# A hybrid mixer layer on one core: branch inputs rounded inside the last inverse transform, branch projections on two sets of banks, arrays placed anew, the vector block loaded ahead of x

## The reference, cut to what matters

```python
h = rmsnorm(x, n1) * (1 + sc1) + sh1
u = h @ w_in                                   # 56 weight tiles of 1024 x 128
z = x1 * (fft_conv(v, kf[:, 0]) + bias[0] * v)  # Hyena, two orders, FFT over the sequence
z = x2 * (fft_conv(z, kf[:, 1]) + bias[1] * z)
y_a = z @ w_a                                  # Hyena branch, 512 channels in
y_b = fnet_branch(u_fn) @ w_b                  # FNet branch, 512 channels in
y_c = ((h_f + h_b) * gelu(u_ry)) @ w_c         # RG-LRU branch, 1024 channels in
x = x + g1 * ((ga * y_a + gb * y_b + gc * y_c) @ w_o)
h = rmsnorm(x, n2) * (1 + sc2) + sh2
x = x + g2 * ((silu(gt) * up) @ w_down)        # FFN
```

## Time and profile before

| what | value |
|---|---|
| median of 3 runs (lowest, highest) | 2621.64 us (2621.34, 2622.27) |
| the profiled execution | 2618.41 us, of which the span of the trace is 2616.5 us |
| PE busy in matmuls | 2477.3 us, 95% of the span |
| DVE, ACT, POOL busy | 55%, 24%, 26% |
| mean granted TensorE clock | 0.978 of full |
| DMA | 24.9% of 16 engines, 90 GB/s mean |

### The profile page before, as it was taken

How to read it: one execution, slowest core, us unless ns; L and a number is a source line. 1 busy time by engine, 2 the same in 40 slices (tenths; PEclk the granted TensorE clock), 3 DMA queues, 4 the chain that set the end, 5 groups by cost and what they waited for, 6 DMA issues and landing times. The chain is left out here.

```text
span 2616.5 us, 34805 instructions
## 1 busy us (share of the span) xinstructions
PE 2477.3 (95%) x13478; PEld 2099.3 (80%) x13478; DVE 1447.0 (55%) x2691; ACT 623.4 (24%) x887; POOL 688.2 (26%) x300
## 2 busy tenths in 40 slices
PE   4599999999997999999979989999999999999997
PEld 2488888867775888888868878888888888888886
DVE  5778786566585777776764383752233322332236
ACT  3423222565664222222220011310000000000004
POOL 1011111221212222322224452433134231432220
PEclk8799999999998999999989999999999999999999
DMA  7144443211115222322354242111011000111002
GB/s 297 48 172 156 166 161 117 82 40 61 60 40 190 99 99 98 116 98 98 118 204 148 66 166 82 49 33 46 19 48 48 32 32 32 48 40 40 24 24 81
DMA packets 53752, 234.24 MB, mean 90 GB/s; under 512 B 6131, under 2 KB 8755, under 8 KB 48068
## 3 DMA queue, kind: packets, MB, share of 16 engines
q1 hardware_dynamic: 53700, 233.54, 24.9%
HBM read 178.98 MB, written 54.53 MB: 89 GB/s over the span
## 5 line engine op out<-in xcount | busy, mean ns | idle before, releaser
L801 PE MATMUL ps<-h_hi,w_hi 128*128 128x512 f32 (+1 forms) x2112 | 760.3, 360 | 15.1 <-DVEq L1718 9.4
L803 PE MATMUL ps<-h_hi,w_lo 128*128 128x512 f32 (+1 forms) x2112 | 750.0, 355 | 0.0
L802 PE MATMUL ps<-h_lo,w_hi 128*128 128x512 f32 (+1 forms) x2112 | 750.0, 355 | 0.0
L759 POOL TENSOR_TENSOR w_hi<-w_raw,zero_col 128x1024 fp32r<-128x1024 f32 x96 | 205.5, 2140 | 1638.4 <-PE ps L803 1198.6
L801 PEld LDWEIGHTS ps<-h_hi,w_hi 128*128 128x128 f32 x2112 | 400.8, 190 | 77.0 <-DVEq L1718 9.8
L803 PEld LDWEIGHTS ps<-h_hi,w_lo 128*128 128x128 f32 x2112 | 400.4, 190 | 57.3
L802 PEld LDWEIGHTS ps<-h_lo,w_hi 128*128 128x128 f32 x2112 | 400.9, 190 | 56.5 <-issue 0.2
L2051 DVE TENSOR_TENSOR a<-sil,ps 128x512 f32<-128x512 f32 (+1 forms) x66 | 39.5, 599 | 504.1 <-PE ps L803 501.8
L762 POOL TENSOR_TENSOR w_lo<-w_raw,w_hi 128x1024 fp32r<-128x1024 f32 x96 | 262.3, 2732 | 7.5
L2074 DVE SCALAR_TENSOR_TENSOR x<-ps,mod,x 128x512 f32<-128x512 f32 (+1 forms) x264 | 172.3, 661 | 98.1 <-PE ps L803 97.5
L802 PE MATMUL ps<-h_lo,wf_hi 128*128 128x512 f32 (+1 forms) x624 | 224.3, 359 | 0.0
(11 more groups left out here) (276 smaller groups left out, 3500.3 us busy)
## 6 DMA issues: line engine op xcount, KB each, us to landing
w_raw<-in_weights SPq DMA_DIRECT2D x146, 512.0 KB, 3.9
ada_w<-in_w_ada SPq DMA_DIRECT2D x18, 1024.0 KB, 8.2
scratch_gate_s<-g_st SPq DMA_DIRECT2D x24, 640.0 KB, 3.3
side<-scratch_gate_s SPq DMA_DIRECT2D x24, 640.0 KB, 4.0
scratch_k_s<-kstage SPq DMA_DIRECT2D x8, 1536.0 KB, 6.6
hy_k<-scratch_k_s SPq DMA_DIRECT2D x8, 1536.0 KB, 8.7
scratch_hy_s<-hout SPq DMA_DIRECT2D x16, 640.0 KB, 3.2
ada_early<-in_w_ada SPq DMA_DIRECT2D x6, 1024.0 KB, 20.7
```

The costliest lines, as they stand in the source:

```text
L759: nc.gpsimd.tensor_tensor(hi[:], w_raw[slot % 2][:], zero_col[:].to_broadcast([P, D]), ALU.add).then_inc(pool_step, 1)
L801: mm(out, w_pair[0], x_pair[0], start=first, stop=False)
L802: mm(out, w_pair[0], x_pair[1], start=False, stop=False)
L803: return mm(out, w_pair[1], x_pair[0], start=False, stop=last)
```

## The change

What it does, part by part:

- **vec ahead of x.** The block of vectors `vec` (81 KB) is issued on SP ahead of the 8 tiles of x, instead of behind them.
- **Norm 1.** DVE multiplies both latent pieces of x by their roots ahead of the conditioning (8 tiles in each of two turns); ACT copies the root of the context piece to SBUF (`rstd_ctx`). So ps[1] and ps[2] come free early, and piece 1 is made as piece 0 is. ACT makes u of tiles 1, 3 and 5 of both latent pieces, DVE the others.
- **Arrays placed anew.** `v_b` and `g_st` lie where they can be written before RG-LRU has ended. `v_b` is loaded behind `inv`, ahead of the last chunk's `zc_ready`, and ACT's gate(0) of the first L3 pass waits for `xr_ready` instead of `zc_ready`; a new semaphore `xr_used` guards `ztok`.
- **z 0 to 3 in the last L3 pass.** The last pass is written apart from the loop on SP, ACT and DVE. SP loads z 2 (into `v_b`) and 3 (into a buffer of its own) behind `hy_k` of the last order, z 0 and 1 where it did, and the gates of jobs 0 and 1 behind the last inverse unit. ACT rounds the four in the order 2, 3, 0, 1 around its copies of the last inverse units, DVE takes their remainders ahead of its last inverse.
- **Two sets of banks.** Odd jobs use ps[3] to ps[5], with semaphores `other_done` and `other_free`. DVE takes job n-4 ahead of z n, where it took z n first.

```diff
+U_BY_ACT = [n < 2 * KD and n % KD in (1, 3, 5) for n in range(3 * KD)]
...
+        Z_ORDER = [2, 3, 0, 1] + list(range(4, 16))
...
+            return (other_free[b], u // 2 + 1) if u % 2 else (proj_free[b], use0 + u // 2 + 1)
...
+            sp.dma_start(vec[:], dr["vec"]).then_inc(vec_in, 16)
             sp.dma_start(x_in[:, 0, :], dr["x"][0]).then_inc(x_loaded[0], 16)
             sp.dma_start(cvec[:], dr["cvec"]).then_inc(cvec_in, 16)
             for k in range(1, KD):
                 sp.dma_start(x_in[:, k, :], dr["x"][k]).then_inc(x_loaded[k], 16)
-            sp.dma_start(vec[:], dr["vec"]).then_inc(vec_in, 16)
...
                         sp.dma_start(inv[:], dr["inv"]).then_inc(hy_const_in, 16)
+                        sp.dma_start(v_b[:], dr["hy_s"][0]).then_inc(v_in, 16)
                     sp.wait_ge(zc_ready, n + 2)
...
-            sp.dma_start(v_b[:], dr["hy_s"][0]).then_inc(v_in, 16)
             sp.dma_start(dr["state_out"], fin[:]).then_inc(fin_stored, 16)
...
+                    if order == 1 and last:
+                        load_z(2, dr["zb_s"][2])
+                        load_z(3, dr["zb_s"][3])
...
                             sp.wait_ge(y_ready, 4 * CH)
-                            for n in range(3):
+                            for n in range(2):
                                 load_z(n, dr["zb_s"][n])
+                            sp.wait_ge(mix_done[LAST_INVERSE[0]], LAST_INVERSE[1])
+                            for n in range(2):
+                                load_side(n, gate_src[n])
...
+            act.wait_ge(proj_done[2], 1)
+            fn(rstd_ctx, ps[2][:, 0:CTX], ACT.Copy).then_inc(proj_free[2], 1)
             act.wait_ge(norm_ready, 1)
...
-                        act.wait_ge(zc_ready, 1 + KD)
+                        act.wait_ge(xr_ready, 1 + KD)
                     gate(0)
 
+                    act.wait_ge(xr_used, KD)
...
                         if j == 2:
                             gate(2, (0,))
+                            if last and order == 1:
+                                round_z(2)
...
+                    if last and order == 1:
+                        for n in Z_ORDER[1:4]:
+                            round_z(n)
                     gate(2, (1, 2))
...
-                for k in ((), (0, 1, 2, 3), (4, 5, 6, 7), ())[r]:
-                    dve.wait_ge(x_loaded[k], 16)
-                    own.add(tt(x_in[:, k, 0:512], x_in[:, k, 0:512], ps[0], ALU.mult))
+                if r in (1, 2):
+                    p = r - 1
+                    a, e, _ = PIECES[p]
+                    dve.wait_ge(proj_done[p], 1)
+                    for k in range(KD):
+                        dve.wait_ge(x_loaded[k], 16)
+                        own.add(tt(x_in[:, k, a:e], x_in[:, k, a:e], ps[p], ALU.mult))
...
+                    if last and order == 1:
+                        dve.wait_ge(mix_done[LAST_INVERSE[0]], LAST_INVERSE[1])
+                        for n in Z_ORDER[0:4]:
+                            split_z(n)
                     for j in range(5):
                         mix_taken(u3, c, j0 + 9 + j)
...
-            for n in range(4):
-                split_z(n)
             for n in range(4, 12):
-                split_z(n)
                 take_branch(n - 4, n - 4)
+                split_z(n)
```

More of the change, by code:

```diff
@@ L388, in build_program @@
         inv = sb(st, "inv", [P, FH, 3, P])
+        v_b = sb(st, "v_b", [P, T])
+        x_b = sb(st, "x_b", [P, T])
         hy_y = sb(st, "hy_y", [P, 20, P])
-        x_b = sb(st, "x_b", [P, T])
-        v_b = sb(st, "v_b", [P, T])
+        g_st = sb(st, "g_st", [P, T])
         z_b = sb(st, "z_b", [P, T])
+        sb(st, "under_ztok", [P, 8])
         ztok = sb(st, "ztok", [P, FH, P])
@@ L463, in build_program @@
         mix_free = [sem(f"mix_free{b}") for b in range(MIX_BANKS)]
+        other_done = [sem(f"other_done{b}") for b in range(3)]
+        other_free = [sem(f"other_free{b}") for b in range(3)]
         act_step, dve_step = sem("act_step"), sem("dve_step")
@@ L666, in load_z, with load_side @@
                 sp.dma_start(buf[:], src).then_inc(loaded, 16)
+            def load_side(n, src):
+                if 2 <= n < 10:
+                    for b in range(3):
+                        sp.wait_ge(*branch_free(n - 2, b))
+                elif n >= 10:
+                    sp.wait_ge(side_used, n - 9)
+                sp.dma_start(side[n % 2][:], src).then_inc(side_in[n % 2], 16)
+            z_src = [dr["zb_s"][c] for c in range(4)] + [dr["zc_s"][n] for n in range(8)] + \
+                    [dr["za_s"][c] for c in range(4)]
+            gate_src = [dr["gate_s"][8 + m] for m in range(8)] + [dr["gate_s"][16 + m] for m in range(8)] + \
+                       [dr["gate_s"][m] for m in range(8)]
             def l3_pass(c, last):
@@ L1388, in _, with round_z, l3_pass @@
                     own.restart()
-            with act.Fori(0, CH) as c:
+            def round_z(n):
+                raw, loaded, count, _ = raw_z(n)
+                act.wait_ge(loaded, count)
+                dst = h_hi[:, n - 4, :] if 4 <= n < 12 else z2_hi[:, n % 12, :]
+                fn(dst, raw[:], ACT.Copy).then_inc(zhi_ready, 1)
+            def l3_pass(c, last):
                 for order in range(2):
@@ L1889, in _, with split_z, l3_pass @@
                     own.restart()
-            with dve.Fori(0, CH) as c:
+            def split_z(n):
+                at = Z_ORDER.index(n)
+                if n == 3:
+                    dve.wait_ge(z_split, at)
+                dve.wait_ge(zhi_ready, at + 1)
+                if 4 <= n < 12:
+                    hi, lo = h_hi[:, n - 4, :], h_lo[:, n - 4, :]
+                else:
+                    hi, lo = z2_hi[:, n % 12, :], z2_lo[:, n % 12, :]
+                tt(lo, raw_z(n)[0][:], hi.bitcast(F32), ALU.subtract).then_inc(z_split, 1)
+            def l3_pass(c, last):
                 for order in range(2):
@@ L1970, in split_merged @@
                 tt(h_lo[:, m, :], x1[:, m, :], h_hi[:, m, :].bitcast(F32), ALU.subtract).then_inc(m_split, 1)
-            for n in range(4):
+            for n in range(4, 12):
+                take_branch(n - 4, n - 4)
                 split_z(n)
-            for n in range(4, 12):
-                split_z(n)
-                take_branch(n - 4, n - 4)
             for n in range(12, 16):
@@ L1981, in _ @@
                 if m == 0:
-                    proj_taken(use0 + 7)
+                    for b in range(3):
+                        dve.wait_ge(*branch_free(7, b))
                 take_branch(8 + m, m)
```

171 lines of the change are left out of this document (89 added, 82 removed).

## The result

| what | value |
|---|---|
| changed kernel, median of 4 runs (lowest, highest) | 2591.54 us (2587.34, 2594.79) |
| kernel before, median of 4 runs beside it | 2621.49 us (2617.76, 2622.27) |
| ratio, 95% interval | 0.9888 (0.9874, 0.9903) |
| the profiled execution, its span | 2594.79 us, 2593.0 us |

What follows compares the result with a forecast made beforehand. PE, busy 2477.3 of 2616.5 us, bounds the kernel, leaving 139.2 idle to remove. Gains 13.4 + 1.5 + 12 + 4 = 30.9 against the median 2621.64 give 2590.7, stated as 2590.5; own range 2583 to 2598, wider range 2579 to 2604.

Steps and rivals of the forecast that it cites:

- Setup, 13.4: Setup up to PE's unit at 122.40: 9.9 from norm_a coming earlier plus 3.6 from piece 1, unit at 109.0.
- 11.5 earlier: Setup: ACT's ada_row starts at 43.9 and not at 55.37, because vec is loaded ahead of x.
- Start of L3, 1.5: Start of L3: the 16.56 wait on v_b goes, but the order's chain takes time back; gain 1.5 to 2, taken 1.5.
- All three links: Start of L3: DVE transforms 8.07 earlier, ACT's copy still held by gate's store, POOL's split costing 4 of 5.5.
- Jobs 0 to 7 and the wide entry, 12: Branch start: 18.3 wait and 1.9 slow clock gained, less 1.5, 3.3 and 2.4, and 1 for favourable estimates.
- Stalls 1.5 and 3.3: Branch start: PE waits 1.5 before job 2 (take behind z_b) and 3.3 before job 3 (behind z 4's remainder).
- The regained 1.9 of clock: Job 0: slow clock of 0.56 over the first 4 us goes with the removed wait, worth 1.9.
- Wide and last narrow jobs, 4: Four waits on side, 3.0 together, go with two sets of banks; with PE's refill 1 wide, 3 last narrow.
- B: Rival: all stalls close, with 10 at the start of L3 and 18 at the branch start; about 2576, chance 0.18.
- D: Rival: slower, load, rounding, remainder and take on each narrow job's path, 8.7 us each; about 2660, chance 0.03.
- C: Rival: setup gives less, terms 8, 0, 10.5 and 4, sum 22.5; 2599, chance 0.15.
- POOL in the inverse: Last inverse: POOL's w_hi blocked until DVE's chain ends, then meeting z_b; by the skill's rule time 2589.7 instead.

Runs made afterwards that it cites:

- v_late: Changed kernel with the first v_b load put back behind the last zc store; 2592.68 us, ratio 0.9896.
- all_three: Changed kernel with first L3 gate's store early, job 1 taken ahead of z 4's remainder, z 11's remainder ahead of job 7; 2576.12 us.
- gate_early: Changed kernel with the first L3 gate's store issued on SP ahead of the wait for zc_ready; 2585.65 us, ratio 0.9874.
- pool_hold: all_three with POOL's third split of the output projection's weights held until DVE has taken the last remainder; 2570.89 us, ratio 0.9811.

## Why the prediction was right, point by point

The forecast was 2590.5; measured were 2591.54 and 2593.32 in two sets of runs.

- **The sum.** Predicted 30.9. The table gives 23.5 and 25.8 for the two profiles; with setup at its mean of 13.0 in place of 9.5 the sum is 27.0. The medians differ by 30.0 and 26.2. Two figures in the working are off by 0.1: 9.9 + 3.6 is 13.5, and (1 - 0.56) x 4 is 1.8 where I put 1.9 for the slow clock. That the first median lies 1.0 from the forecast is in part luck: the kernel before read 2621.49 beside it and 2619.1 to 2619.7 in the later sets, and three of the four terms were off by 1 to 3, to either side, as follows.
- **Setup, 13.4.** 13.0 on average, 9.5 in the first profile. `vec` 11.4 and norm 1 1.6, against 11.5 and 2.0 by the prediction's own steps (the row 11.5 earlier; eight products a turn cost 1.6, piece 1 gives 3.6). In the first profile the step that failed is "11.5 earlier": `ada_row` came at 47.16, 8.2 earlier, 2.0 of the missing 3.3 because 20 matmuls for the sum of squares took 4.43 and not 2.39. PE's first unit, for which I named 109.0, started at 112.16. The second `reduce_angle` took 3.02 for 6.62, ahead of POOL, as said, and piece 1 gave 3.5 for 3.6. I had taken PE's own durations from before, where they hold a clock that isn't the same in each execution.
- **Start of L3, 1.5.** -0.3. All three links were there, and the inverse unit started at 853.36; setup gave 3.9 less than forecast, so that is 849.5 on the prediction's clock, for 849.2. The step that failed is the last: a wait of 7.68 in place of 0.27 ahead of the inverse unit brings the slow clock (0.50 for 4 us, some 2.0), which I had counted only as regained. The 1.6 gained at the unit are -0.3 at the next milestone.
- **Jobs 0 to 7 and the wide entry, 12.** 14.0 - 5.0 = 9.0. Job 0 18.3 earlier: right. Stalls 1.5 and 3.3: measured 1.93 and 2.13, for the reasons given. Mis-sized is the wide entry: 3.65 of wait and 1.4 of slow clock for 2.4, as POOL's split of the next tile met the remainder (2.94 for 1.49). The regained 1.9 of clock was spent again behind job 3's stall.
- **Wide and last narrow jobs, 4.** 0.6 + 4.5 = 5.1, of which 0.8 is PE's shorter wait at the output projection (3.7 for 4.5 in all), which I hadn't counted. It doesn't follow from the two sets alone: the last sum took 3.03 in before and 1.49 in changed, but 3.03 in v_late too, which gives 0.6 + 3.2 = 3.8.
- **Rivals.** B's 10 at the start of L3 was there for the taking, but only with the store moved, and not each time (8.8 in all_three, 3.5 and 3.2 in gate_early and pool_hold). D didn't come: load, rounding and remainder of the next z cost one stall of 2.13, at job 3. C's terms came nearest in the first profile: it had 8, 0, 10.5 and 4, sum 22.5, and that profile gave 9.5, -0.3, 9.0 and 5.1, sum 23.5. What speaks for the forecast is its setup term, 13.4 for an average of 13.0; C's setup was one end of a spread, and came at least in part by PE's longer matmuls.
- **POOL in the inverse.** I let POOL's `w_hi` be blocked until the chain ended. The chain in the changed kernel:

```profile
1303.92 0.28 DVE L219 TENSOR_TENSOR ztok<-hy_a 128x128 f32<-128x128 f32 x1
1304.12 0.22 DVE L225 TENSOR_SCALAR hy_a<-hy_a 128x128 f32<-128x128 f32 x1
1304.26 1.98 DVE L228 SCALAR_TENSOR_TENSOR hy_a<-hy_a 128x128 f32<-128x128 f32 x1
1306.16 0.21 DVE L225 TENSOR_SCALAR hy_a<-hy_a 128x128 f32<-128x128 f32 x1
1306.30 2.49 DVE L228 SCALAR_TENSOR_TENSOR hy_a<-hy_y,hy_a 128x128 f32<-128x128 f32 x1
```

POOL asked at 1302.83 and ended at 1306.09. Counted back by its 1.9 it began at 1304.2, at the first operation with one input (L225, 1304.12), and it ended 8 us ahead of the chain's end at 1314.0; in before it asked in a stretch that held only two-input operations, and got in when that ended. The Trainium skill, SBUF — State Buffer, section Who interferes with whom, says that DVE instructions with at most one SBUF input do not contend, as long as they are outside the 2-port perf modes. The trace agrees in so far as POOL got in at such an operation; no row shows in which mode it ran. That one input is not enough by itself is seen in setup, where a one-input operation took 2.40 beside POOL's split in before, and 0.83 in changed, ahead of POOL:

```profile
49.20 2.40 DVE L1613 TENSOR_SCALAR arg<-arg 128x1280 f32<-128x1280 f32 x1
```

```profile
38.83 0.83 DVE L1679 TENSOR_SCALAR arg<-arg 128x1280 f32<-128x1280 f32 x1
```

By the "issue order" of the same section POOL should have got in behind one operation of DVE. At the output projection of v_late it did (asked at 1514.73, in at about 1516.1, as the sum ended); in the chain of short operations it waited 1.3 us, through six of them. The cost moved from `z_b` (1.68 here, 5.11 in the earlier trace rows) into the chain (1.98 and 2.49 for 0.29 each), so `z_b` ended at 1317.5 all the same, within 0.3 of the forecast on this clock.

## What to carry to other kernels

Price a removed wait by the chain that ends next, and look in it for a store: an early load was worth 0 until a buffer's store was moved, and then 3.9 to 9.5. A small new stall can cost TensorE about 1.5 us more than it lasts (2.13 and 3.65 here, each with some 4 us of slow clock behind; 1.93 had it in one kernel and not in another), so look at which new waits an edit brings and not only at the one it removes. After an edit that moves a stage, look at what GpSimd's weight splits now meet: holding one back until vector work that TensorE waits for was done gave 5.

## What the runs showed that was not expected

- Setup takes up to 7 us more or less from one execution to the next with the same code, with the time that PE takes while the roots are formed (six matmuls 4.61 or 2.40). In nine of the eleven profiles the granted clock goes with it (0.56 to 0.65 or 1.00 from 48 to 54 us). In changed and all_three the granted clock reads 1.00 over the stretch in which the six took 4.61; why is open.
- The race of split and products at the start of L3 has two outcomes, 5.3 to 5.6 apart, for 1.5 us of difference in PE's arrival. One kernel has one profile here (the changed one two), so how often each outcome comes isn't known. It goes with the clock: PE's wait of 3.44 ahead of the forward units is followed by 4 us at 0.59 in gate_early, and by 1.00 in changed, where the next wait, of 3.17, is followed by 0.61; in all_three the two groups of forward units took 5.62 and 5.34, in gate_early 7.25 and 3.83. What decides which wait the clock falls behind is open.
- Job 2's wait of 1.93 is left. Taking job 0 ahead of `z_b` should remove it, but `x1` lies where `x_b` is still to be read; that wasn't tried.
